# Modulation product: float32 matmuls against two rounded passes of split weights with stacked condition columns

## The chip, the cores and the metric

The kernel runs on one core of one Trainium2 chip. The metric is the device time of one execution in microseconds (us). The time before is the median of three runs, 3209.94 us (3209.03 to 3211.54).

## The reference, cut to what matters

The reference is a stack of transformer-like layers over 256 latent tokens and 256 context tokens of width 1024 (neighbourhood attention with mLSTM, RWKV, MLPs, and further blocks). The part at issue is the modulation of each of the first two layers:

```python
def modulate(x, shift, scale):
    return rms_norm(x) * (1.0 + scale) + shift

def adaln(cond, w, b):          # w: 1024 x 6144, one per layer
    return jnp.split(jax.nn.silu(cond) @ w + b, 6, axis=-1)
```

There are two conditions, `c` and `c_ctx`, so the product per layer is 2 x 1024 times 1024 x 6144. Its six pieces are shift, scale and gate of the mixer and of the MLP. Only the first layer's first 2048 columns (shift and scale of the mixer) are needed at the start; the rest is needed from the output projection of the first mixer on.

## The kernel before, in words

**Weights.** All weights pass through a ring of three slabs in SBUF (`ring`, 128 x 4096 each), filled by SyncE's queue in the order of the list `slabs`; a slab is loaded when the one three places ahead is used (L3308). A slab of the modulation is 1024 x 512: eight k of 128 rows. Layer 0 has 12 of them (`plan_ada(0, 0, 4)`, then behind the eight slabs of the input projection `plan_ada(0, 4, 8)`), layer 1 has 12.

**The modulation product.** `ada_matmuls` (L798) is a generator that a caller advances with `fill(pe, queue, n)`. One step is one k of one slab: a float32 matmul with the silu of the conditions as the stationary operand (8, 16 or 24 columns: the two condition columns stand in a field of zeros, `csil`, so that slab i writes rows 2i and 2i+1 of one PSUM bank) and 512 columns of weights moving (L812). The profile records such a float32 matmul as two. There are three parts (`ADA_PARTS`, L794): part 0 is layer 0's first four slabs, part 1 its other eight, part 2 layer 1's twelve. When a part is done, ScalarE copies the rows (`ada_rows_act`, L830), TensorE turns them by transposes (`ada_turn_pe`, L841), DVE copies them into `modcol` (L851), and GpSimd stores the rows to DRAM (`ada_store_pool`, L860) from which the gates are loaded as broadcasts.

**Where the steps stand.** Part 0 stands at the start, around the first norms (L3321 on). Part 1 is filled in two steps at a time behind each of the 32 units of the two attentions, `na` (16 neighbourhood units of 512 keys) and `cx` (16 context units of 256 keys). Then follow 24 steps of part 2 in one go (L3335), and its other 72 are filled into the mLSTM stage (`ml_pe`, L1442), two behind each S and two behind each of its 32 steps.

**Attention.** Each engine runs the units in software-pipelined ticks (`unit_tick`): in tick i TensorE does scores of unit i (L1086), the turn of unit i-2 (L1094), values of unit i-3 (L1106), and the fill; DVE does the maximum of unit i (L1128 and L1130, with bias L1143, L1138 and L1147) and normalises unit i-1 (L1155, L1159); ScalarE does the exponential of unit i (L1186), copies unit i-2 (L1205) and puts out unit i-3 (L1237). Each engine works its own list strictly in the order written.

**Between.** The softplus of the gates (`softplus_act`, L1308) starts a chain of small scans on DVE (`decay_dve`), exponentials (`decay_act`), transposes and small matmuls (`decay_pe`, L1379 and L1385), then the transposes of q and k and the mLSTM.

**mLSTM.** Four heads. A head starts with the score matrix S (L1449), two broadcasts M (L1455), the decay matrices on DVE (L1506) and their exponentials, masks and weights (L1514, L1518). Then eight steps (four chunks in two directions) follow: three matmuls each on TensorE (L1466, L1467, L1469), and on DVE the state update (L1534, for the first three chunks) and the output (L1537 to L1554). Into the last head DVE and ScalarE split the first slab of the output projection (L1664, L1669).

**Rounded passes.** The other products of the stage are already done with rounded float32: ScalarE copies a slab into a rounded `high`, DVE subtracts to get a rounded `low` in the ring's place, and TensorE does three rounded matmuls where the float32 one stood (`ab_high_act` L911, `ab_low_dve` L916, `ab_in_pe` L954).

Of the kernel before, what the change touches and what calls it, by code (L numbers as in the profile page):

```python
# [1 line left out]

# [5 lines left out]
ALU = mybir.AluOpType  # L8
# [6 lines left out]
P = 128  # L15
# [15 lines left out]
def constant_blocks():  # L31
# [6 lines left out]
        "ident": p == f,  # L38
        "headones": (p // 64) == (f // 64),
# [67 lines left out]
def bidir_dual_stack(nc, a, out, scratch_mod, scratch_rpb, noted):  # L107
    const_at, n_const = constant_columns()

    with ExitStack() as ctx:  # L110
# [592 lines left out]
        csil = area(23136, KT, 46)  # L703
        pad = arena[0:56, 23000:23127]
# [16 lines left out]
        def setup_pool(pool):  # L721
            nc.gpsimd.memset(csil, 0.0).then_inc(*up(pool, "csil zero"))
            pool.wait_ge(*latest(pool))
            nc.gpsimd.dma_start(x[:, :, :], a["x"][0].rearrange("(t p) d -> p t d", p=P))\
                .then_inc(landing("x"), 16)
            nc.gpsimd.dma_start(cx[:, :, :], a["ctx"][0].rearrange("(t p) d -> p t d", p=P))\
                .then_inc(landing("ctx"), 16)
            for part, (layer, n0, ns, base) in enumerate(ADA_PARTS):
                for v in range(2):
                    nc.gpsimd.dma_start(adab[base + v:base + 2 * ns:2, :],  # L730
                                        a["ada_b"][layer, 512 * n0:512 * (n0 + ns)].rearrange("(i f) -> i f", f=512))\
                        .then_inc(landing(f"ada_b {part}"), 16)
# [37 lines left out]

        def setup_pe(pe):
# [14 lines left out]
        def setup_act(act):  # L786
            act.wait_ge(*when(("read", ("vec", 1))))
            act.wait_ge(*when("csil zero"))
            for i, name in enumerate(("c", "c_ctx")):
                nc.scalar.activation(csil[:, :, 22 + i], colB[:, ROWS_B[name]:ROWS_B[name] + 8], ACT.Silu).then_inc(*up(act, "silu c"))  # L790
                act.wait_ge(*latest(act))


        ADA_PARTS = ((0, 0, 4, 64), (0, 4, 8, 32), (1, 0, 12, 0))  # L794
        ADA_BANK = (2, 6, 0)

        def ada_matmuls(pe, part):
            layer, n0, ns, base = ADA_PARTS[part]  # L798
            rows = psum[0:2 * ns, ADA_BANK[part], :]
# [5 lines left out]
            at = slice(base, base + 2 * ns)  # L805
            nc.tensor.matmul(rows, ident[at, at], adab[at, :], start=True, stop=False)
            for i in range(ns):
                name = (f"ada{layer}", n0 + i, 0)
                for k in range(KT):
                    stage(pe, "ada")  # L810
                    s = slab(pe, name)
                    ins = nc.tensor.matmul(rows, csil[:, k, 22 - 2 * i:22 - 2 * i + 2 * ns], s[:, k, :],  # L812
                                           start=False, stop=(i == ns - 1 and k == KT - 1))
                    if k == KT - 1:
                        event = ("ada", "full", part) if i == ns - 1 else None
                        ins.then_inc(*up(pe, event))
# [2899 lines left out]
```

## Time and profile before

| | before |
|---|---|
| median of three runs | 3209.94 us |
| the profiled execution: its own time | 3208.53 us |
| its span | 3206.7 us |
| TensorE busy (matmuls) | 3001.3 us, 94% |
| DVE busy | 1740.6 us, 54% |
| ScalarE busy | 1084.0 us, 34% |
| GpSimd busy | 315.8 us, 10% |
| DMA | 409.30 MB, mean 128 GB/s |

The profile is of one execution, whose own time is 1.4 us under the median. The span is what the profiler saw of it. The stages at issue, in us from the span's start: start and first modulation part to 52, input projection to about 219, `na` units from 224 to 304, `cx` units to 362, scans and turns to about 402, mLSTM to 525, merge and output projection to about 583. Matmuls overlap in the records, so the distance between starts, not the duration, is what one costs in a row.

### The profile page before, as it was taken

How to read it: one execution, taken by the hardware profiler on the slowest of the kernel's cores; microseconds unless marked ns; L12 is line 12 of the kernel's file. 1: busy time of each engine (PE TensorE's matmuls, PEld its weight loads, DVE VectorE, ACT ScalarE, POOL GpSimd, SP SyncE). 2: the span in 40 equal slices, each digit the busy share in tenths (PEclk: the TensorE clock that was granted, in tenths of full speed). 3: DMA queues.
4: the chain of work that ended last, by engine and by line, in shares of the span. 5: the costliest groups of instructions: out<-in, count | busy, mean ns of one | idle time of the engine just before them, and what ended most of it. 6: DMA issues, size and time to landing. Idle time of an engine off the chain costs nothing. (4 is left out here: it accounts for less than half of the span.)

```text
span 3206.7 us, 55619 instructions
## 1 busy us (share of the span) xinstructions
PE 3001.3 (94%) x24656; PEld 2366.2 (74%) x24656; DVE 1740.6 (54%) x2730; ACT 1084.0 (34%) x1704; POOL 315.8 (10%) x421
## 2 busy tenths in 40 slices
PE   7999988999998978898989999999899999998999
PEld 3864335899985458888949989865699898455898
DVE  3334367656554057878735555445655554565553
ACT  2233302334331234344223343423443333143432
POOL 2320011000000032323210000000000000200000
PEclk9999999999999989999989999999899999999999
DMA  8323534355553010000044555543245555413353
GB/s 260 100 105 105 184 131 140 124 184 185 193 176 119 26 28 3 3 3 3 19 143 158 191 164 181 185 147 131 80 158 178 176 185 172 151 60 131 101 183 138
DMA packets 250489, 409.30 MB, mean 128 GB/s; under 512 B 10455, under 2 KB 103016, under 8 KB 250120
## 3 DMA queue, kind: packets, MB, share of 16 engines
q1 hardware_dynamic: 245128, 390.39, 35.8%
q0 software_dynamic: 5120, 15.35, 1.9%
q8 instruction: 194, 3.18, 0.4%
q14 instruction: 47, 0.39, 0.0%
HBM read 400.67 MB, written 2.95 MB: 126 GB/s over the span
## 5 line engine op out<-in xcount | busy, mean ns | idle before, releaser
L350 DVE TENSOR_TENSOR ring_parts<-ring,arena_parts 128x2048 fp32r<-128x2048 f32 (+1 forms) x262 | 580.2, 2255 | 276.9 <-ACT arena_parts L343 274.4
L343 ACT CAST arena_parts<-ring 128x2048 fp32r<-128x2048 f32 (+1 forms) x262 | 480.5, 1885 | 521.7 <-PE psum L2701 229.5
L2701 PE MATMUL psum<-arena_parts 128*128 128x256 f32 x2816 | 513.4, 285 | 2.1 <-DVE arena_parts L575 1.7
L2701 PEld LDWEIGHTS psum<-arena_parts 128*128 128x128 f32 x2816 | 444.6, 194 | 3.5 <-DVE arena_parts L575 2.8
L2701 PE MATMUL psum<-arena_parts,ring_parts 128*128 128x256 f32 x1408 | 401.2, 285 | 0.0
L387 PE MATMUL psum<-arena_parts 128*128 128x512 f32 x1024 | 327.1, 393 | 2.0 <-DVE arena_parts L575 2.0
L2701 PEld LDWEIGHTS psum<-arena_parts,ring_parts 128*128 128x128 f32 x1408 | 273.3, 194 | 0.0
L1737 PE MATMUL psum<-arena_parts 128*128 128x512 f32 x768 | 236.8, 389 | 0.0
L387 PEld LDWEIGHTS psum<-arena_parts 128*128 128x128 f32 x1024 | 193.9, 190 | 42.9 <-DVE arena_parts L575 2.7
L387 PE MATMUL psum<-ring_parts,arena_parts 128*128 128x512 f32 x560 | 219.6, 392 | 0.0
L1719 PE MATMUL psum<-arena_parts 128*128 128x256 f32 x1024 | 195.6, 294 | 5.3 <-issue 3.2
L812 PE MATMUL psum<-ring,arena 128*24 128x512 f32 (+2 forms) x384 | 185.9, 618 | 2.6 <-DMA ring<-in_ada_w 2.6
L1719 PEld LDWEIGHTS psum<-arena_parts 128*128 128x128 f32 x1024 | 166.5, 200 | 9.6 <-issue 6.1
L1737 PEld LDWEIGHTS psum<-arena_parts 128*128 128x128 f32 x768 | 143.4, 188 | 29.0
L2732 DVE TENSOR_TENSOR sc<-sc,psum 128x512 f32<-128x512 f32 x44 | 30.2, 687 | 226.0 <-PE psum L2701 226.0
L1737 PE MATMUL psum<-ring_parts,arena_parts 128*128 128x512 f32 x384 | 149.4, 389 | 0.0
L1719 PE MATMUL psum<-arena_parts,ring_parts 128*128 128x256 f32 x512 | 148.8, 291 | 0.0
L498 POOL TENSOR_SCALAR stat<-stat 128x1 f32<-128x1 f32 x26 | 9.0, 347 | 1327.2 <-ACT sc L489 1327.2
L3202 PE MATMUL psum<-ring,hT 128*128 128x512 f32 x256 | 126.0, 622 | 1.0 <-DMA ring<-in_xmem_wkv 1.0
L387 PEld LDWEIGHTS psum<-ring_parts,arena_parts 128*128 128x128 f32 x560 | 106.3, 190 | 22.4
L2325 PE MATMUL psum<-ring,hT 64*64 64x64 f32 x2560 | 106.8, 234 | 16.1 <-POOL ring L2296 11.8
L2325 PEld LDWEIGHTS psum<-ring,hT 64*64 64x64 f32 x2560 | 99.3, 149 | 17.4 <-POOL ring L2296 11.9
(466 smaller groups left out, 5596.3 us busy)
## 6 DMA issues: line engine op xcount, KB each, us to landing
ring<-in_mlp_w SPq DMA_DIRECT2D x48, 2048.0 KB, 8.3
ring<-in_ada_w SPq DMA_DIRECT2D x24, 2048.0 KB, 7.9
ring<-in_ffn_pre_w_gu SPq DMA_DIRECT2D x44, 1024.0 KB, 6.9
ring<-in_ffn_post_w_gu SPq DMA_DIRECT2D x44, 1024.0 KB, 7.0
ring<-in_ffn_pre_w_down SPq DMA_DIRECT2D x8, 2048.0 KB, 7.8
ring<-in_xmem_wkv SPq DMA_DIRECT2D x8, 2048.0 KB, 7.9
ring<-in_ffn_post_w_down SPq DMA_DIRECT2D x8, 2048.0 KB, 7.9
ring<-in_ab_w_in SPq DMA_DIRECT2D x7, 2048.0 KB, 7.7
```

The lines of the kernel that those rows point to most:

```text
L343: nc.scalar.copy(high_view(name)[:, k, :], raw_view(name)[:, k, :]).then_inc(*up(act, ("high", name, h)))
L350: nc.vector.tensor_tensor(low_view(name)[:, k, :], raw_view(name)[:, k, :], high_view(name).bitcast(F32)[:, k, :], ALU.subtract)\
L387: ins = nc.tensor.matmul(psum[:, b, :], lhs[q][:, k0 + k, P * t:P * t + P], s[:, k, :], start=(k0 + k == 0 and i == 0), stop=(k0 + k == kt ...
L498: nc.gpsimd.tensor_scalar(s[:, 4 + t:5 + t], s[:, 2 * t:2 * t + 1], s[:, 2 * t + 1:2 * t + 2], EPS, ALU.add, ALU.add).then_inc(*up(pool))
L812: ins = nc.tensor.matmul(rows, csil[:, k, 22 - 2 * i:22 - 2 * i + 2 * ns], s[:, k, :], start=False, stop=(i == ns - 1 and k == KT - 1))
L1719: ins = nc.tensor.matmul(psum[:, b, 256 * j:256 * j + 256], s[:, k, at:at + P], src[q][:, k, :], start=(k == 0 and i == 0), stop=(k == 7 a ...
L1737: ins = nc.tensor.matmul(psum[:, b, :], hid_groups[g % 2][q][:, k, P * t:P * t + P], s[:, k, :], start=(g == 0 and k == 0 and i == 0), sto ...
L2325: ins = nc.tensor.matmul(psum[h, b, 64 * c:64 * c + 64], B[left][z][h, c, :], B[right][z][h, c, :], start=True, stop=True)
L2701: ins = nc.tensor.matmul(psum[:, b, 256 * j:256 * j + 256], s[:, k, at:at + P], x_parts[q][:, k, :], start=(k == 0 and i == 0), stop=(k == ...
L2732: nc.vector.tensor_tensor(t, t, psum[:, 2 * (n % 2) + 1, :], ALU.mult)\
L3202: ins = nc.tensor.matmul(psum[:, 6 + i, :], hT[:, k, 256 + P * i:256 + P * i + P], s[:, k, :], start=(k == 0), stop=(k == KT - 1))
```

## The change

The product of parts 1 to 3 is made of rounded weights, in two passes (high and low). The silu is split too, and its high and low columns are stacked: four stationary columns per slab instead of two (`csil_parts`), so that each slab writes four rows, and a small matmul with a constant 0/1 matrix `pairsum` adds the pairs and turns them at once. Part 0 keeps its float32 matmuls. Layer 1's slabs are regrouped: its first four are now part 2, its last eight part 3. A step is now a quarter slab (two k): ScalarE copies the quarter into one of four (later two) buffers, DVE subtracts, TensorE does four matmuls. 48 quarters (12 slabs) go into the attentions, alternately one and two behind a unit; 32 quarters (8 slabs) into the mLSTM stage, one behind each step; the 24 steps between are gone.

```diff
+        ADA_PARTS = ((0, 0, 4, 0), (0, 4, 8, 32), (1, 0, 4, 0), (1, 4, 8, 64))
+        ADA_BANK = (2, 6, 7, 0)
+        ADA_FIRST = (None, 0, 32, 48)
...
+        def ada_high_act(act, g):
+            held = stages[act.name]
+            stage(act, "ada_split")
+            act.wait_ge(*when(("slab", slab_at[ada_slab(g)])))
+            if g < 4:
+                act.wait_ge(*when(("qk", "turned", 7)))
+            elif g < 48:
+                act.wait_ge(*when(("ada quarter", g - 4)))
+            elif g < 50:
+                act.wait_ge(*when("gate columns full"))
+            else:
+                act.wait_ge(*when(("ada quarter", g - 2)))
+            nc.scalar.copy(ada_high_at(g), ada_quarter(raw_view, g)).then_inc(*up(act, ("ada high", g)))
+            stage(act, held)
+        def ada_low_dve(dve, g):
...
+            dve.wait_ge(*when(("ada high", g)))
+            nc.vector.tensor_tensor(ada_quarter(low_view, g), ada_quarter(raw_view, g),
+                                    ada_high_at(g).bitcast(F32), ALU.subtract).then_inc(*up(dve, ("ada low", g)))
+        def ada_ahead(u):
+            return range(min(48, 3 * u // 2 + 4), min(48, 3 * (u + 1) // 2 + 4))
+        def ada_each(u):
+            return 3 * (u + 1) // 2 - 3 * u // 2
...
+                        for j in range(2):
+                            for w in (high, low):
+                                ins = nc.tensor.matmul(rows, csil_parts[:, 2 * q + j, live], w[:, j, :], start=False,
+                                                       stop=last and j == 1 and w is low)
```

The turn of a part, the sum of its pairs for the store in DRAM, and where the splits stand in the lists of the engines:

```diff
-                ins = nc.tensor.transpose(psum[:, b, 2 * ns * j:2 * ns * j + 2 * ns], adab[at, P * j:P * j + P], ident[at, at])
+                ins = nc.tensor.matmul(psum[:, b, 2 * ns * j:2 * ns * j + 2 * ns], adab[at, P * j:P * j + P],
+                                       cst("pairsum")[at, 0:2 * ns], start=True, stop=True)
...
+        def ada_sum_pe(pe, part, b):
...
+            nc.tensor.matmul(psum[0:2 * ns, b, :], cst("pairsum")[at, 0:2 * ns], adab[at, :], start=True, stop=True)\
+                .then_inc(*up(pe, ("sum", "full", part)))
...
             def out(i):
                 att_out(act, key, units, i)
+                if split is not None:
+                    for g in ada_ahead(split + i):
+                        ada_high_act(act, g)
...
+                for g in range(48 + 8 * h, 56 + 8 * h):
+                    ada_high_act(act, g)
+                    if g in (75, 77):
+                        ab_out_high_act(act, 0, g // 77)
+                        stage(act, "ml")
...
                         b = 4 + z + 2 * (j % 2)
+                        ada_low_dve(dve, 48 + 8 * h + 2 * j + z)
```

TensorE's, ScalarE's and DVE's lists:

```diff
-            att_pe(pe, "na", na, [("read", ("qkT", i)) for i in range(8)], ada[1], 2)
-            att_pe(pe, "cx", cxa, (), ada[1], 2)
-            fill(pe, ada[1], 1)
-            fill(pe, ada[2], 24)
+            ada_next = chain(ada[1], ada[2])
+            att_pe(pe, "na", na, [("read", ("qkT", i)) for i in range(8)], ada_next, ada_each)
+            att_pe(pe, "cx", cxa, (), ada_next, ada_each)
+            fill(pe, ada_next, 1)
+            ada_turn_pe(pe, 1, 2)
+            ada_turn_pe(pe, 2, 3)
+            ada_sum_pe(pe, 1, 0)
...
-            att_act(act, "na", na, 0.125, [("ab_in", "full", 6, 3)])
-            att_act(act, "cx", cxa, 0.125)
-            ada_rows_act(act, 1)
+            att_act(act, "na", na, 0.125, [("ab_in", "full", 6, 3)], split=0)
+            att_act(act, "cx", cxa, 0.125, split=16)
             softplus_act(act)
+            for part in (1, 2):
+                ada_rows_act(act, part)
+            ada_sum_act(act, 1, 0)
...
-            att_dve(dve, "na", na, 0.125, after_first=["bias ready"])
-            att_dve(dve, "cx", cxa, 0.125)
+            att_dve(dve, "na", na, 0.125, after_first=["bias ready"],
+                    split=lambda i: ([i] if i < 4 else []) + (list(ada_ahead(i - 3)) if i >= 3 else []))
+            for g in ada_ahead(13):
+                ada_low_dve(dve, g)
+            att_dve(dve, "cx", cxa, 0.125, split=lambda i: ada_ahead(14 + i))
```

In the attentions DVE's `split(i)` stands behind the normalisation of unit i, which is in tick i+1; ScalarE's high copies stand behind the output of unit i, in tick i+3 (and those of quarters 0 to 3 behind the first four exponentials). In `ml_pe` the fill behind S is gone and the one behind each step is one quarter. `decay_out_dve` is followed by the `modcol` copies of parts 1 and 2, the turn of part 3 with its sum stands where both turns stood, ahead of the second half of the output projection. At the start, `x` is loaded ahead of the memset of `csil`, `adab` is cleared and its bias rows loaded for parts 0, 1 and 3 (part 2's later, `late_bias_pool`), the silu goes to `stat` and is split by ScalarE and DVE. The buffer `pad` of the position bias moves to another place, for which ScalarE waits ahead of the outputs of one projection slab that the bias rows have been written.

## Rows read from the trace of the kernel before

**Rows 1.** The page: busy us of each engine, share of the span, instructions.
```profile
PE 3001.3 (94%) x24656; PEld 2366.2 (74%) x24656; DVE 1740.6 (54%) x2730; ACT 1084.0 (34%) x1704; POOL 315.8 (10%) x421
```
**Rows 2.** Busy by stretch: length, PE, PEld, DVE, ACT, POOL, clock, DMA share, GB/s.
```profile
120.00:160.00 40.00, 40.00 (x174) 32.35 (x173) 17.75 (x19) 11.95 (x12) 14.00 (x16) 1.00 0.17 55
240.00:291.00 51.00, 51.00 (x202) 20.81 (x200) 24.03 (x55) 17.05 (x44) 5.05 (x12) 0.99 0.24 83
312.75:353.50 40.75, 40.75 (x145) 14.51 (x144) 13.67 (x50) 12.38 (x48) 0.00 (x0) 1.00 0.35 118
362.40:383.20 20.80, 20.79 (x49) 4.87 (x48) 15.43 (x45) 3.52 (x5) 1.15 (x2) 1.00 0.86 301
404.70:525.00 120.30, 109.36 (x377) 44.54 (x376) 84.32 (x278) 12.25 (x13) 17.07 (x25) 0.94 0.41 141
535.60:544.90 9.30, 4.81 (x25) 3.36 (x25) 8.57 (x24) 6.34 (x17) 2.23 (x4) 0.61 0.17 62
```
**Rows 3.** Timeline, neighbourhood attention, DVE: start us, us, engine, line, operation [idle before].
```profile
246.49 0.42 DVE L1143 SCALAR_TENSOR_TENSOR sc<-psum,arena 128x256 f32<-128x256 f32 x1 [2.16 <-PE psum L1086]
...
248.33 0.49 DVE L1159 TENSOR_SCALAR sc<-sc,stat 128x512 f32<-128x512 f32 x1
250.97 0.42 DVE L1143 SCALAR_TENSOR_TENSOR sc<-psum,arena 128x256 f32<-128x256 f32 x1 [2.15 <-PE psum L1086]
```
**Rows 4.** Timeline, context attention, one tick of all engines.
```profile
312.75 0.70 PE L1086 MATMUL psum<-arena 64*128 64x256 f32 x2
...
313.55 0.42 DVE L1128 TENSOR_REDUCE stat<-psum 128x1 f32<-128x256 f32 x1 [4.04 <-PE psum L1086]
...
314.19 0.47 ACT L1186 ACTIVATE sc<-psum,stat 128x256 f32<-128x256 f32 x1 [4.24 <-DVE stat L1130]
314.32 1.89 PE L812 MATMUL psum<-ring,arena 128*16 128x512 f32 x4
314.39 0.35 DVE L1159 TENSOR_SCALAR sc<-sc,stat 128x256 f32<-128x256 f32 x1
...
314.66 0.36 ACT L1205 COPY sc<-psum 128x256 f32<-128x256 f32 x1
314.91 0.26 ACT L1237 COPY hT<-psum 64x128 f32<-64x128 f32 x1
316.14 0.70 PE L1086 MATMUL psum<-arena 64*128 64x256 f32 x2
```
**Rows 5.** Timeline, mLSTM stage, DVE in one step and the next one's start.
```profile
418.83 0.35 DVE L1534 SCALAR_TENSOR_TENSOR sc<-sc,psum 128x129 f32<-128x129 f32 x1 [0.60 <-PE psum L1469]
...
420.57 0.35 DVE L1554 SCALAR_TENSOR_TENSOR arena<-sc,stat,arena 128x128 f32<-128x128 f32 x1
...
421.52 0.35 DVE L1534 SCALAR_TENSOR_TENSOR sc<-sc,psum 128x129 f32<-128x129 f32 x1 [0.60 <-PE psum L1469]
```
**Rows 6.** Timeline, mLSTM stage, DVE from the start of the second head.
```profile
435.33 2.16 DVE L1506 TENSOR_SCALAR arena<-psum,sc 128x128 f32<-128x128 f32 x8 [3.29 <-PE psum L1455]
...
440.82 0.35 DVE L1534 SCALAR_TENSOR_TENSOR sc<-sc,psum 128x129 f32<-128x129 f32 x1
```
**Rows 7.** Lines L916 and L911, the splits of the input projection: duration ns min/median/max, shapes.
```profile
L916 DVE TENSOR_TENSOR ring_parts<-ring,sc_parts x7: 2291/2292/2293, 47.1 to 184.3; 128x2048 fp32r<-128x2048 f32 x7
L916 DVE TENSOR_TENSOR ring_parts<-ring,ring_parts x1: 1226/1226/1226, 182.5 to 182.5; 128x1024 fp32r<-128x1024 f32 x1
...
L911 ACT CAST ring_parts<-ring x1: 1050/1050/1050, 181.4 to 181.4; 128x1024 fp32r<-128x1024 f32 x1
```
**Rows 8.** Timeline: the last fill and the softplus, and two turns on TensorE.
```profile
359.62 1.89 PE L812 MATMUL psum<-ring,arena 128*16 128x512 f32 x4
...
362.15 0.63 ACT L1308 ACTIVATE arena<-arena 4x512 f32<-4x512 f32 x1
...
391.03 3.55 PE L1385 MATMUL psum<-arena,const 4*128 4x4 f32 x16
...
52.04 0.41 PE L841 MATMUL psum<-const,adab 8*128 8x8 f32 x4 [0.66 <-ACT adab L830]
```

More of the change, by code:

```diff
@@ L769, in bias_pool, with ada_bias_pool, late_bias_pool @@
             pool.wait_ge(*latest(pool))
+        def ada_bias_pool(pool, part):
+            layer, n0, ns, base = ADA_PARTS[part]
+            for v in range(2):
+                nc.gpsimd.dma_start(adab[base + v:base + 4 * ns:4, :],
+                                    a["ada_b"][layer, 512 * n0:512 * (n0 + ns)].rearrange("(i f) -> i f", f=512))\
+                    .then_inc(landing(f"ada_b {part}"), 16)
+        def late_bias_pool(pool):
+            stage(pool, "bias")
+            layer, n0, ns, base = ADA_PARTS[2]
+            pool.wait_ge(*when(("mod", "turned", 0)))
+            nc.gpsimd.memset(adab[base:base + 4 * ns, :], 0.0).then_inc(*up(pool))
+            pool.wait_ge(*latest(pool))
+            ada_bias_pool(pool, 2)
         def setup_pe(pe):
@@ L808, in ada_matmuls @@
                 name = (f"ada{layer}", n0 + i, 0)
-                for k in range(KT):
+                live = slice(28 - 4 * i, 28 - 4 * i + 4 * ns)
+                for q in range(4):
                     stage(pe, "ada")
[L811 to L816, printed above, removed]
-                        now[("used", slab_at[name])] = (f"ada_by_{pe.name}", count[f"ada_by_{pe.name}"])
+                    last = i == ns - 1 and q == 3
+                    if part == 0:
+                        s = slab(pe, name)
+                        for k in (2 * q, 2 * q + 1):
+                            ins = nc.tensor.matmul(rows, csil[:, k, live], s[:, k, :], start=False, stop=last and k == 7)
+                    else:
+                        g = ADA_FIRST[part] + 4 * i + q
+                        pe.wait_ge(*when(("ada low", g)))
+                        high, low = ada_high_at(g), ada_quarter(low_view, g)
+                        for j in range(2):
+                            for w in (high, low):
+                                ins = nc.tensor.matmul(rows, csil_parts[:, 2 * q + j, live], w[:, j, :], start=False,
+                                                       stop=last and j == 1 and w is low)
+                    if part or q == 3:
+                        ins.then_inc(*up(pe, ("ada", "full", part) if last else None))
+                        here = (f"ada_by_{pe.name}", count[f"ada_by_{pe.name}"])
+                        if part:
+                            now[("ada quarter", g)] = here
+                        if q == 3:
+                            now[("used", slab_at[name])] = here
                     yield
@@ L1112, in att_pe, with att_dve @@
                 if queue is not None and step is values:
-                    fill(pe, queue, each)
-        def att_dve(dve, key, units, scale, probs=True, after_first=(), mem_after={}, rows=None):
+                    fill(pe, queue, each if isinstance(each, int) else each(i))
+        def att_dve(dve, key, units, scale, probs=True, after_first=(), mem_after={}, rows=None, split=None):
             stage(dve, "att")
@@ L1166, in att_dve @@
                     stage(dve, "att")
+                if step is normalise and split is not None:
+                    for g in split(i):
+                        ada_low_dve(dve, g)
                 if step is normalise and rows is not None and i in (5, 7):
@@ L1171, in att_dve, with att_act @@
                     out_low_dve(dve, rows, k, 2)
-        def att_act(act, key, units, scale, needs=(), rows=None):
+        def att_act(act, key, units, scale, needs=(), rows=None, split=None):
             stage(act, "att")
@@ L3321, in _ @@
             setup_pe(pe)
-            ada = [ada_matmuls(pe, part) for part in range(3)]
-            fill(pe, ada[0], 16)
+            ada = [ada_matmuls(pe, part) for part in range(4)]
+            fill(pe, ada[0], 8)
             first_turn_pe(pe, "L0a")
-            fill(pe, ada[0], 8)
+            fill(pe, ada[0], 4)
             first_turn_pe(pe, "C0a")
-            fill(pe, ada[0], 8)
+            fill(pe, ada[0], 4)
             fill(pe, ada[0], 1)
```

93 lines of the change are left out of this document (63 added, 30 removed).

## The prediction

> **What bounds the kernel now.** I read the page first: TensorE is busy 94% of the span, VectorE (DVE) 54% [rows 1]. That is a mean over stages, so the second view was the busy time by stretch. The change acts between 224 and 545 us of the span, and the stretches there differ [rows 2]. In both attentions and in the mLSTM stage TensorE is (nearly) always busy and DVE waits; between 362 and 383 us TensorE works off 24 modulation steps while the decay scans on DVE set the pace. The third view was the timeline of one period of each stage. A neighbourhood unit repeats every 4.48 us, with DVE idle for 2.15 of them [rows 3]. A context unit repeats every 3.39 us, of which 1.82 are the two modulation steps [rows 4]. An mLSTM step repeats every 2.69 us, of which 1.71 are two modulation steps, and DVE idles only 0.60 [rows 5]. So what matters is how much TensorE time goes and how much DVE time comes, stage by stage, against idle times of 2.15, 2.2 and 0.60 us.
>
> **Prices.** An old step is two records of 0.43 us (49 in 20.8 us) [rows 2]: 0.86 us. A rounded matmul of 512 columns costs 0.23 us (174 in 40 us) [rows 2], so a quarter slab (two k, high and low: four matmuls) costs 0.92 us where its two old steps cost 1.71. All 20 slabs free 63 us of TensorE. Each quarter adds a rounded copy of 128x1024 on ScalarE, 1.05 us, and a subtraction of 128x1024 on DVE, 1.226 us [rows 7]. In a row of instructions a subtraction takes between 1.04 (its columns alone: 2291 less 1226 ns for 1024) and 1.26 (its duration and the 0.04 between dependent instructions of [rows 5]). I take 1.15, since neighbours don't depend on it. 80 of them are 92 us of DVE.
>
> **Neighbourhood attention.** DVE per unit is 2.38 us (246.49 to 248.33, and 0.49 and the gap) and 1.5 subtractions: 4.1 us. TensorE is 4.48 less 1.82 and plus 1.38: 4.0 us. DVE becomes the pace, narrowly: 0.37 less a unit over 11 steady units, -4.1 us. The last units, where TensorE is alone, save 2.0 (four fills of 1.82 against six quarters); the start at half clock, where ScalarE has four early copies ahead of its own work, saves 0.6. Sum -6.7 us (-8 to -4).
>
> **Context attention.** This is the part that decides. DVE's list for tick t is maximum t, normalise t-1, then the subtractions of `ada_ahead(14 + t - 1)`. ScalarE's is exponent t (waits for maximum t), copy t-2, output t-3, then the high copies of `ada_ahead(16 + t - 3)`: the same quarters. In the first attention DVE asks for them one tick later (`i - 3`); here in the same tick. So maximum t+1 stands behind a subtraction, which waits for a high copy, which stands behind exponent t, which waits for maximum t: a ring through two in-order engines. From [rows 4]: maximum to exponent 0.64, to the copy 0.47, to the output 0.25, its 0.26, then 1.05 for the high copy and about 0.06 of signals: 2.74 us a tick, and 1.15 for each subtraction. Ticks with one quarter take 3.9 us, with two 5.0. Thirteen such ticks with 19 quarters are 57.5 us; the three ahead of them about 6.6, the end (normalise, turn, values, one quarter) 3.1: 67 us, where sixteen units took 54.2 and about 0.9 for a cold start. +12 us. If the ring didn't bind, DVE's own work would be 1.2 and 1.73, 3.0 a unit, and the stage would gain 4.
>
> **Between the stages.** The 24 steps at 362 us go, 20.8 us of TensorE, and bring nothing: DVE's scans (15.4 us busy in that stretch) [rows 2] and the exponentials after them hide them. Into that cover come the row copies, turns and sum of parts 1 and 2, an estimated 8 us of TensorE even at half clock; without the scans they would cost those 8. The softplus no longer waits for the last fill and the row copy: 359.62 to 362.15 [rows 8] becomes about 0.4, -2.1 us. The fill between the first S and M goes, on the path into the first head: -1.8 us.
>
> **mLSTM.** TensorE per step falls to 0.86 and 0.92, 1.8 us. DVE's list per step is 2.1 us (418.83 to 420.57, and 0.35) [rows 5] and one subtraction: 3.25. 32 steps, less 0.38 in the eight that update no state: 101 us. DVE's work at a head's start is 5.5 (435.33 to 440.82) [rows 6], four times 22; four `cat` remainders 2.9; two `ab_out` remainders 4.5; at three head changes DVE waits some 0.3 for M, 1 in all. 131.4 us against 120.3 [rows 2]: +11.1 us (+7 with 1.04 a subtraction, +15 with 1.26). ScalarE's copies are no term: each waits for the quarter two before it and has over 2 us to spare. Behind the new waits on DVE nothing stands but the state update, needed by TensorE two steps on.
>
> **Edges.** The turns become full matmuls. Eight such took 3.55 us at half clock, 0.44 each, so about 0.22 at full clock: four cost 0.9 against 0.41 for the first transposes [rows 8], +0.5. Ahead of the second half of the output projection stand turns and a sum of 512 columns, in a stretch at clock 0.61 [rows 2], of which part would else run cold: +1.0 (0 to 2). TensorE enters `ab_out` later beside DVE's merge: +0.3. Setup (x issued ahead of the memset, four bias loads for six, another memset) lies before the first slab has landed: 0. The late bias load and the wait for the bias rows come tens of us before anyone needs them: 0. Slabs are used every 10 to 13 us, where the old fills used one in 6.9 without a stall (8 steps at 0.86, the stretch from 362.4 of rows 2): 0.
>
> **Clock.** With TensorE idle a third of the time in two stages some of it will run at 1.2 GHz. The mLSTM stage shows 0.94 at 91% busy, the first attention 0.99 at full [rows 2]. At half clock throughout, a context tick costs 5.7 instead of 4.5 and an mLSTM step 3.6 instead of 3.1: 34 us. I take 2 (0 to 34).
>
> **Sum:** -6.7 + 12 - 2.1 - 1.8 + 11.1 + 0.5 + 1.0 + 0.3 + 2 = +16.3 us. The profiled execution took 3208.53 us (span 3206.7), 1.4 under the median of 3209.94; I add to the median: 3226 us.
>
> **Rivals.**
> - *The ring doesn't bind*: some cover lets the high copies run ahead, and DVE's throughput sets the context attention. Then that part is -4 and the sum 0: 3210 us. For it, ScalarE is idle 70% there; against it, the order of both lists. 0.12.
> - *Faster: the subtraction runs at the rate of one-source operations.* L1159 takes 0.49 us for 512 columns [rows 3] and 0.35 for 256 [rows 4], 0.55 ns a column, which makes 0.77 for 1024, 0.69 in a row. 51 subtractions on the path (32 and 19) save 0.46 each, 23 us: 3203 us. It decides below 0.83 us a subtraction, and is faster beyond noise only below 0.71. Against it, the same kind of instruction shows 1.226 [rows 7]. With smaller ways to gain, 0.09.
> - *Half clock*: TensorE's gaps of 1 to 2 us in each tick keep it at 1.2 GHz for most of both stages: 3258 us, for half of them 3241. For it, the clock is already 0.61 in the stretch that is half idle [rows 2]; against it, work at half clock fills the gaps. 0.12.
> - *No cheaper matmul*: with few stationary columns a rounded matmul takes 0.43 us like a half of the old. A quarter is then 1.7 us, a neighbourhood unit 5.2 instead of 4.1, 16 us more, and the other stages hide it: 3242 us. 0.05.
>
> On the second rival: the trace shows 1.20 ns a column for two tensors. The Trainium skill (VectorE: DVE Perf Modes, "Why `tensor_tensor` can't do 2×_2P or 4×") says that the doubled mode spends the second read port on the same tensor, so an operation of two tensors can't have it. By that rule this rival falls away; the trace agrees. On the third: the Trainium skill (TensorE: Matmul & The Clock Gate, "A second HAM failure mode: psum-queue depth-cycling") tells of a kernel whose short idle times between groups of matmuls made the clock swing. By that rule the time would lie nearer to 3241; no run here shows it yet.
>
> **How the numbers follow.** My case has 0.60 and a range of its own of 3217 to 3237. With the ring's rival at 3210 and half of the clock's at 3241 the range is 3208 to 3242; outside stay the faster case and the full half clock. A measurement tells about 0.2%, 6.4 us. Faster: 0.09. Within: the ring's rival and the low end of mine, 0.16. Slower: 0.75.
>
> **What would show it.** Right: context ticks of 3.9 and 5.0 us in turn, DVE waiting for ScalarE's high copy about 1.5 us in each, softplus some 4 us later than 362; the mLSTM stage 131 us with DVE over 90% busy; neighbourhood units of 4.1 us. Wrong: context ticks near 3.0 (no ring), mLSTM steps of 2.7 or less (cheap subtractions) or 3.6 with a clock near 0.5, and anything moved behind the output projection, where both traces should run alike.

## The result and the profile after

The changed kernel takes 3228.0 us (median of four runs, 3227.9 to 3231.7) against 3209.5 us for the kernel before beside it (3208.7 to 3211.5): ratio 1.006, 95% interval 1.0048 to 1.0072. It is 18.5 us slower; the forecast was 16.3 us slower.

The profiled execution of the changed kernel is the longest of its four, 3231.74 us (span 3229.9), 3.7 us over their median; experiment 2 shows where such a difference can lie. The page's busy times, and the group of all new subtractions (busy, mean ns; idle time before them):

```profile
PE 2964.4 (92%) x24682; PEld 2384.8 (74%) x24682; DVE 1833.4 (57%) x2813; ACT 1165.9 (36%) x1788; POOL 326.0 (10%) x425
...
L853 DVE TENSOR_TENSOR ring_parts<-ring,arena_parts 128x1024 fp32r<-128x1024 f32 x80 | 97.5, 1234 | 26.8 <-ACT arena_parts L846 25.1
```

TensorE lost 36.9 us of busy time and VectorE gained 92.8 [rows 1]; the span grew all the same. Busy time by stretch, to be read against [rows 2] (length, PE, PEld, DVE, ACT, POOL, granted clock, DMA share, GB/s). The four are the neighbourhood attention, the ring part of the context attention, the scans, the mLSTM:

```profile
224.00:302.40 78.40, 75.80 (x325) 37.95 (x324) 64.87 (x105) 52.34 (x93) 22.36 (x39) 0.87 0.41 142
309.00:371.00 62.00, 53.35 (x186) 22.30 (x185) 36.15 (x74) 32.91 (x74) 0.00 (x0) 0.78 0.39 136
375.40:396.40 21.00, 6.19 (x26) 3.25 (x23) 15.42 (x45) 6.85 (x9) 1.14 (x2) 0.60 0.41 147
415.20:547.20 132.00, 81.22 (x362) 50.92 (x361) 120.84 (x310) 43.87 (x44) 21.32 (x24) 0.86 0.32 112
```

In the context attention no engine is full: TensorE 86%, VectorE 58%, ScalarE 53%. In the mLSTM VectorE is at 92%, TensorE at 62%; before, VectorE was at 70% and TensorE at 91% [rows 2]. The same points in both traces, the first row in us from the span's start, show where the time came from. A unit's maximum is the first instruction of VectorE on it, the first D is the first decay matrix of the mLSTM, and the merge is what follows its last step:

| from ... to | before | after | difference | forecast |
|---|---|---|---|---|
| start to first maximum of `na` | 225.5 | 224.7 | -0.8 | +0.5 |
| first maximum of `na` to that of `cx` | 79.5 | 77.8 | -1.7 | -6.7 |
| first maximum of `cx` to softplus | 57.1 | 72.9 | +15.8 | +12 - 2.1, and 2 for the clock |
| softplus to first D | 42.6 | 39.8 | -2.8 | -1.8 |
| first D to merge | 120.2 | 132.1 | +11.9 | +11.1 |
| merge to the end | 2681.7 | 2682.6 | +0.9 | +1.3 |

The sum, taken before rounding, is 23.2 us in these two executions, 4.7 more than between the medians.

One tick of the context attention, VectorE and ScalarE alone (start us, us, engine, line, operation [idle before <- who ended it]):

```profile
327.72 0.42 DVE L1228 TENSOR_REDUCE stat<-psum 128x1 f32<-128x256 f32 x1
...
328.36 0.47 ACT L1289 ACTIVATE sc<-psum,stat 128x256 f32<-128x256 f32 x1 [2.07 <-DVE stat L1230]
328.56 0.35 DVE L1259 TENSOR_SCALAR sc<-sc,stat 128x256 f32<-128x256 f32 x1
...
329.08 0.26 ACT L1345 COPY hT<-psum 64x128 f32<-64x128 f32 x1
329.24 1.05 ACT L846 CAST arena_parts<-ring 128x1024 fp32r<-128x1024 f32 x1
330.39 1.23 DVE L853 TENSOR_TENSOR ring_parts<-ring,arena_parts 128x1024 fp32r<-128x1024 f32 x1 [1.48 <-ACT arena_parts L846]
331.53 0.42 DVE L1228 TENSOR_REDUCE stat<-psum 128x1 f32<-128x256 f32 x1
```

ScalarE idles 2.07 us for VectorE's maximum and VectorE 1.48 us for ScalarE's high copy. This is the chain of the forecast. The tick is 3.81 us, where it was 3.39 us in [rows 4]. The next lines are VectorE in two mLSTM steps and the start of a third. VectorE shows no idle time at all (0.60 us a step in [rows 5]), and the steps take 3.19 and 3.39 us:

```profile
453.11 1.23 DVE L853 TENSOR_TENSOR ring_parts<-ring,arena_parts 128x1024 fp32r<-128x1024 f32 x1
454.25 0.34 DVE L1646 SCALAR_TENSOR_TENSOR sc<-sc,psum 128x129 f32<-128x129 f32 x1
...
456.30 1.23 DVE L853 TENSOR_TENSOR ring_parts<-ring,arena_parts 128x1024 fp32r<-128x1024 f32 x1
...
459.69 1.23 DVE L853 TENSOR_TENSOR ring_parts<-ring,arena_parts 128x1024 fp32r<-128x1024 f32 x1
```

### The profile page after: what moved, and what is told of

Read it like the earlier page. It is cut to its first block and busy times, and to the rows that moved or that the text cites. A ratio compares the mean times of both kernels' runs of the same rounds, so it can differ in the third digit from the quotient of the medians.

```text
span 3229.9 us, 55857 instructions
## 1 busy us (share of the span) xinstructions
PE 2964.4 (92%) x24682; PEld 2384.8 (74%) x24682; DVE 1833.4 (57%) x2813; ACT 1165.9 (36%) x1788; POOL 326.0 (10%) x425
## 5 line engine op out<-in xcount | busy, mean ns | idle before, releaser
L389 PEld LDWEIGHTS psum<-arena_parts 128*128 128x128 f32 x1024 | 192.9, 189 | 42.6 <-DVE arena_parts L577 2.7
L2437 PE MATMUL psum<-ring,hT 64*64 64x64 f32 x2560 | 104.4, 230 | 17.1 <-POOL ring L2408 11.9
L853 DVE TENSOR_TENSOR ring_parts<-ring,arena_parts 128x1024 fp32r<-128x1024 f32 x80 | 97.5, 1234 | 26.8 <-ACT arena_parts L846 25.1
```

Source lines behind the costliest of these rows:

```text
L389: ins = nc.tensor.matmul(psum[:, b, :], lhs[q][:, k0 + k, P * t:P * t + P], s[:, k, :], start=(k0 + k == 0 and i == 0), stop=(k0 + k == kt ...
L853: nc.vector.tensor_tensor(ada_quarter(low_view, g), ada_quarter(raw_view, g), ada_high_at(g).bitcast(F32), ALU.subtract).then_inc(*up(dve, ...
L2437: ins = nc.tensor.matmul(psum[h, b, 64 * c:64 * c + 64], B[left][z][h, c, :], B[right][z][h, c, :], start=True, stop=True)
```

## The experiments

**1. The ring opened (`cx_later`).** One edit in VectorE's list: in the context attention the subtractions that make the low parts (the remainders) come one tick later.

```diff
             for g in ada_ahead(13):
                 ada_low_dve(dve, g)
-            att_dve(dve, "cx", cxa, 0.125, split=lambda i: ada_ahead(14 + i))
+            att_dve(dve, "cx", cxa, 0.125, split=lambda i: ada_ahead(13 + i) if i else ())
+            for g in ada_ahead(29):
+                ada_low_dve(dve, g)
```

> In the context attention VectorE subtracts each quarter's remainder one step of the loop later than in the changed kernel (the remainders of a tick no longer wait for the high copies that ScalarE makes in the same tick), everything else as in the changed kernel. Theory (the ring through VectorE and ScalarE paces the ticks at 3.8 and 4.9 us): the ticks fall to what the busiest engine needs, VectorE's 1.5 x 1.23 + 1.3 = 3.2 us a tick, so the stretch from the fourth maximum to the last normalisation falls from 62.3 to about 44 us and the whole by 12 to 19 us, to 3209 to 3216. Rival A (TensorE at half clock paces it, not the ring): TensorE was busy 53.4 of 62.0 us there at a mean granted clock of 0.78, so no more than 9 us can go, to about 3220 or above. Rival B (the time is paid again later, in the softplus and the gate rows that follow): the attention falls, the whole stays at 3228.

Measured: 3212.4 us (11 runs, 3206.9 to 3215.8), ratio to the kernel before 1.0001 (0.9992 to 1.001): 15.6 us under the changed kernel. The stretch from the fourth maximum to the last normalise fell from 62.3 to 41.0 us, and first maximum to softplus from 72.9 to 48.8. The stretch in the trace:

```profile
307.20:347.90 40.70, 40.70 (x185) 18.56 (x185) 37.55 (x75) 32.34 (x73) 0.00 (x0) 1.00 0.65 226
```

TensorE is busy throughout, at full clock: 40.7 us of busy time in place of 53.4 for the same matmuls (185 and 186 records). The difference, 12.7 us, is what the half clock had cost in busy time. In one tick of it the subtraction no longer waits, and ScalarE waits 0.17 us for the maximum where it waited 2.07:

```profile
326.42 0.47 ACT L1289 ACTIVATE sc<-psum,stat 128x256 f32<-128x256 f32 x1 [0.17 <-DVE stat L1230]
326.62 0.35 DVE L1259 TENSOR_SCALAR sc<-sc,stat 128x256 f32<-128x256 f32 x1
...
327.05 2.36 DVE L853 TENSOR_TENSOR ring_parts<-ring,arena_parts 128x1024 fp32r<-128x1024 f32 x2
```

It follows that the order of one list made the context attention's loss. The stretch differs between executions, but not by so much: with the ring open it took 41.0, 42.5 and 45.1 us in the other three profiled executions (`hybrid_again`, `hybrid_start`, `hybrid`, granted clock 1.00, 0.97 and 0.91), with the ring closed never less than 59.3. Rival A is out: its bound of 9 us took TensorE's busy time for fixed, but the half clock went with the waits. Rival B is out in the stages that follow: first D comes 24.2 us earlier, and so does the merge. Between the two profiled executions 24.1 us are left at the merge and 18.3 at the end; 3.5 of the difference goes between 1240 and 1620 us of the span, where the two kernels run the same instructions. It is of the size of the spread between executions: from the merge to the end one and the same kernel took 2682.8 us in `hybrid` and 2686.2 in `hybrid_again`. What it comes from is open.

**2. More work for TensorE in the same ring (`cx_high_twice`).** The added passes spoil the product; they are a load and nothing else.

```diff
-                            for w in (high, low):
+                            for w in ((high, high, low) if 24 <= g < 48 else (high, low)):
```

> In the context attention each high pass is issued twice, so a quarter has 6 matmuls in place of 4 (the product of that part is then not the reference's; a load on TensorE alone). It asks whether TensorE fell to half clock there because it had too little to do. Theory (the ring leaves TensorE idle, its clock falls, and the half clock costs about 4 us): with 48 more matmuls of 0.21 us at full clock the mean granted clock of the stretch rises from 0.78 to over 0.95, the ticks come down to the ring's 3.8 and 4.9 us and the stretch of 62.3 us stays or falls to about 58. Rival (the clock does not follow the load so closely, TensorE is the bound at half clock): 48 matmuls of 0.43 us make the stretch longer by 10 to 20 us.

Measured: 3227.0 us in one run. From the fourth maximum to the last normalise, where the changed kernel took 62.3 us:

```profile
303.60:364.20 60.60, 55.07 (x222) 23.90 (x221) 36.18 (x74) 33.00 (x73) 0.00 (x0) 0.89 0.40 139
```

Half again as many passes, and the stretch is no longer than before: TensorE was not the bound, and the rival's 10 to 20 us did not come. The last ticks alternate between 3.81 or 4.07 and 5.16 or 5.21 us. The granted clock is 0.89 against 0.78, not the 0.95 of the theory, and whether the added passes raised it is not shown. The changed kernel's own instructions were profiled in this stretch three times more, in `part3_float`, `ml_half_one_source` and `ml_half_gpsimd`, whose edits act later: 59.4, 59.3 and 62.3 us, at 0.87, 0.87 and 0.77. The first of them:

```profile
309.64:369.00 59.36, 47.93 (x186) 20.75 (x185) 36.41 (x74) 32.95 (x74) 0.00 (x0) 0.87 0.41 142
```

So 60.6 us at 0.89 lies within what the kernel does without the added passes. What these executions do show is the price of the clock in the ring: the three ticks from the ninth maximum on take 17.4 us at 0.60 in the changed kernel's profile and 14.5 at 0.98 in `part3_float`, 2.9 us that are there in two executions of four. The three unprofiled executions of the changed kernel are 3.6 to 3.8 us shorter than its profiled one, which would fit with the shorter form, but they left no trace.

**3. No remainders at all (`no_low`).**

```diff
-                        pe.wait_ge(*when(("ada low", g)))
+                        pe.wait_ge(*when(("ada high", g)))
...
-                            for w in (high, low):
+                            for w in (high,):
...
         def ada_low_dve(dve, g):
...
-            nc.vector.tensor_tensor(ada_quarter(low_view, g), ...
```

> All remainders and their passes are left out (the modulation product from the high parts alone, so 2 matmuls a quarter and no subtraction); the high copies stay. It shows by stage what the remainders cost. By my theory: neighbourhood attention from 4.16 us a unit to about 3.7 (TensorE's own work and ScalarE's copies), 5 to 8 us less in the stage; context attention without the ring, ticks about 3 us, 15 us less or more; mLSTM steps from 3.25 to 2.1 us, 32 x 1.15 = 37 us less; about 55 to 60 us in all, 3168 to 3173. Rival (the cost lies in the waits on the high copies and in the half clock): mLSTM falls by less than 20 us and the context attention by less than 6, since less matmul work also lowers the clock, 3190 or above.

The product is then made of the high parts alone. Measured: 3151.1 us in one run, 77 under the changed kernel, where 55 to 60 were expected. The context attention (fourth maximum to last normalise) and the mLSTM (first D to merge):

```profile
294.50:327.00 32.50, 31.46 (x144) 14.49 (x144) 14.45 (x55) 31.06 (x72) 0.00 (x0) 1.00 0.83 291
...
371.30:466.20 94.90, 66.58 (x325) 49.50 (x324) 84.18 (x279) 45.66 (x45) 14.85 (x24) 0.82 0.50 175
```

The mLSTM falls by 37.3 us, 1.16 for each of 32 subtractions: the price of 1.15 taken in the forecast, on the path in full. The low passes are gone too, but they are not what counts there: `hybrid` below puts TensorE's work back in another form, and the stage takes 93.7 us. The first maximum of `na` to that of `cx` falls from 77.8 to 65.4 us, more than the 5 to 8 expected: the units alternate between 3.25 and 3.70 us, which is 7.0 of it, the start gives 3.3 and the end 2.1. From there to the softplus it falls by 33.0 us, where 15 or more were expected. How subtractions and passes share in these two was not tested. The rival is out.

**4. Half of the mLSTM's remainders on GpSimd (`ml_half_gpsimd`).**

```diff
-                        ada_low_dve(dve, 48 + 8 * h + 2 * j + z)
+                        if z == 0:
+                            ada_low_dve(dve, 48 + 8 * h + 2 * j + z)
...
                         pool.wait_ge(*latest(pool))
+                for g in range(49 + 8 * h, 56 + 8 * h, 2):
+                    ada_low_pool(pool, g)
```

`ada_low_pool` is `ada_low_dve` with `nc.gpsimd.tensor_tensor`.

> In the mLSTM every second quarter's remainder (those of the backward steps, 16 of 32) is subtracted by GpSimd instead of VectorE. Theory (VectorE paces the 32 steps at 3.25 us and each subtraction costs it 1.15 us on the path): the stretch from the first D to the merge falls by 16 x 1.15 = 18 us, from 132.1 to about 114, and the whole to about 3210. Rival A (VectorE is not the pace, TensorE's wait on the state is): nothing moves, 3228. Rival B (GpSimd's subtraction slows VectorE's own instructions while both run, or is itself late): GpSimd takes about 2.5 us for one (10.1 us for 4096 elements a row in the trace of the kernel before), four a head, 10 of about 30 us; if VectorE's instructions beside it grow by a fifth, 18 us shrink to about 5 to 10, 3218 to 3223.

Measured: 3245.8 us (four runs, 3240.4 to 3246.7), ratio 1.0104 (1.0089 to 1.012): 18 us slower than the changed kernel, where no theory went above 3228. First D to merge is 145.6 us instead of 132.1, and these 13.5 us are all but 0.5 of what lies between the two profiled executions. Timeline, GpSimd and VectorE:

```profile
470.75 0.16 DVE L1669 RECIPROCAL stat<-stat 128x1 f32<-128x1 f32 x1
...
470.91 2.34 POOL L861 TENSOR_TENSOR ring_parts<-ring,arena_parts 128x1024 fp32r<-128x1024 f32 x1 [2.34 <-ACT arena_parts L846]
470.95 2.45 DVE L1677 SCALAR_TENSOR_TENSOR arena<-sc,stat,arena 128x128 f32<-128x128 f32 x1
473.43 1.22 DVE L853 TENSOR_TENSOR ring_parts<-ring,arena_parts 128x1024 fp32r<-128x1024 f32 x1
```

The sum into the arena, 0.35 us otherwise, takes 2.45 and ends 0.15 us after GpSimd's subtraction. Over the stage three of VectorE's kinds of instruction grew by more than 0.2 us, all with two operands in SBUF: the subtraction by 8.9, the sum into the arena by 8.4 and the 128x1 comparison by 7.0 us, 24.3 together (the text recorded ahead of experiment 5 has 22.6). That is more than the 16 x 1.23 us that GpSimd took over, but by 4.6 us only. Besides, VectorE now waits 10.0 us for TensorE ahead of its state updates, where it waited 0.3, and the granted clock of the stage is 0.74 instead of 0.86; what of that follows from what was not separated. Those of the steps that read PSUM kept their durations to 0.01 us. The Trainium skill (SBUF — State Buffer, "SBUF: two separate sides") says that VectorE and GpSimd share a port pair that one of them holds for a whole instruction, and that a VectorE instruction with two inputs in SBUF needs it, but only against a GpSimd instruction that reads SBUF. By that rule rival B was the one to expect, and larger than I priced it; the trace agrees.

**5. The same with one source on GpSimd (`ml_half_one_source`).**

```diff
-            nc.gpsimd.tensor_tensor(ada_quarter(low_view, g), ada_quarter(raw_view, g),
-                                    ada_high_at(g).bitcast(F32), ALU.subtract)
+            nc.gpsimd.tensor_scalar(ada_quarter(low_view, g), ada_quarter(raw_view, g),
+                                    0.0, None, ALU.mult)
```

> As ml_half_gpsimd, but GpSimd multiplies the raw quarter by 0 in place of subtracting the high part (one source in SBUF in place of two; the low passes of those quarters then add nothing). It asks what held VectorE up in ml_half_gpsimd, where three of its kinds of instruction grew and no other: the subtraction (median 1.23, up to 3.26 us), the 128x1 comparison (0.16, up to 1.40) and the sum into the arena (0.35, up to 2.45), each with two operands in SBUF, 22.6 us together. Theory (a VectorE instruction with two operands in SBUF is shut out while GpSimd reads SBUF at all): the same three kinds still grow, for as long as the shorter GpSimd instruction lasts, the stretch from first D to merge ends between 114 and 146 us. Rival (only two readers of two sources each collide): no instruction of VectorE grows, and the stretch falls to about 114 us, the whole to about 3210.

The low parts of these quarters are then zero. Measured: 3226.5 us in one run; first D to merge 127.0 us, 5.1 less than in the changed kernel. GpSimd and VectorE in two places:

```profile
432.48 3.06 POOL L861 TENSOR_SCALAR ring_parts<-ring 128x1024 fp32r<-128x1024 f32 x1 [2.34 <-ACT arena_parts L846]
...
434.17 0.16 DVE L1667 TENSOR_TENSOR stat<-stat,sc 128x1 f32<-128x1 f32 x1
...
434.56 1.05 DVE L1674 TENSOR_SCALAR arena<-sc,stat 128x128 f32<-128x128 f32 x1
...
437.88 3.69 POOL L861 TENSOR_SCALAR ring_parts<-ring 128x1024 fp32r<-128x1024 f32 x1 [2.35 <-ACT arena_parts L846]
...
440.21 0.35 DVE L1677 SCALAR_TENSOR_TENSOR arena<-sc,stat,arena 128x128 f32<-128x128 f32 x1
```

My theory falls for the short instructions. The comparison at 434.17 and the sum at 440.21, each with two operands in SBUF, run at their usual 0.16 and 0.35 us in the middle of GpSimd's instruction. What is held up is VectorE's one-source instruction from SBUF to SBUF (L1674): 0.29 us otherwise, here 1.05, ending with GpSimd's at 435.6. It grew by 3.0 us in all. Whether GpSimd's subtraction holds it up too is not shown: in `ml_half_gpsimd` none of them began inside one. Of the two-operand ones only the long ones grew: the first subtraction of each head, begun 0.42 us after GpSimd's instruction, takes 1.69 us and ends 0.66 before it, and a subtraction of 128x2048 for the output projection takes 3.12 us instead of 2.28. It holds in the other direction too: GpSimd's instruction takes 2.77 us at its shortest and 3.69 at 437.88, where VectorE's subtraction had begun just before it. The same section of the Trainium skill has a VectorE instruction with two inputs in SBUF blocked by any GpSimd instruction that reads SBUF, for its full length; on this point the measurement differs. The stretch did not come down to the rival's 114 either. GpSimd's one-source instruction takes 3.16 us on average, not 2.59, and TensorE waited for it 11 times, 9.2 us; how the rest divides stays open.

**6. The last part back to float32 (`hybrid`, `part3_float`).** `hybrid` has the edit of `cx_later`, and part 3 is multiplied as in the kernel before, in 64 steps of one k, placed as follows; `part3_float` has the same without the edit of `cx_later`.

```diff
-                    if part == 0:
+                    if part in (0, 3):
...
             fill(pe, ada_next, 1)
+            fill(pe, ada[3], 6)
             ada_turn_pe(pe, 1, 2)
             ada_turn_pe(pe, 2, 3)
-            ada_sum_pe(pe, 1, 0)
+            ada_sum_pe(pe, 1, 4)
+            fill(pe, ada[3], 14)
             decay_pe(pe)
...
                     nc.tensor.matmul(psum[:, 2 + z, :], sel[0:4, h, :], gm[0:4, z, :], ...
+                fill(pe, queue, 3)
...
-                for g in range(48 + 8 * h, 56 + 8 * h):
-                    ada_high_act(act, g)
...
-                        ada_low_dve(dve, 48 + 8 * h + 2 * j + z)
```

> The context attention as in cx_later, and the last part of the modulation product (the eight slabs multiplied beside the mLSTM) goes back to 64 float32 matmuls on the raw slabs: no high copies, no remainders there; 6 of them right after the attention, 14 ahead of the gate columns, 3 in each head's wait for its masks and one in each step. Theory (the changed kernel's mLSTM is paced by VectorE's 32 subtractions, and the kernel before it by TensorE's 72 float32 matmuls of 0.85 us): with 32 to 44 of these and no subtraction neither binds, the stretch from the first D to the merge falls from 132 to what no_low showed without remainders, 95 us; the softplus to D stretch grows by 0 to 3; the whole is 3212 - 37 + 2 = 3177 (3172 to 3185). Rival (TensorE's float32 matmul in each step lies on the state's path, since VectorE waits for the product behind it): 32 x 0.85 = 27 us come back, about 122, 3204.

> The changed kernel with the last part alone put back to float32 (as in hybrid), the context attention's ring left in. If ring and mLSTM are separate costs, it stands above hybrid by what cx_later gained over the changed kernel, 16 us: about 3193. Rival (part of the gain of one was given back by the other, by way of the slab loads): the difference is under 10 us.

Measured: `hybrid` 3170.7 us (3168.7 to 3171.6), ratio 0.9877 (0.9861 to 0.9894), and once more on another occasion (`hybrid_again`, below) 3170.0, ratio 0.9869 (0.9855 to 0.9884). That is 39 us under the kernel before and 57 under the changed one. `part3_float` 3188.1 us (3186.4 to 3192.2), ratio 0.9935 (0.992 to 0.995), 17.4 above `hybrid`, where 16 was expected: ring and mLSTM are separate costs. First D to merge is 93.7 us; its stretch, and the period of VectorE's steps:

```profile
392.50:483.50 91.00, 84.97 (x332) 38.88 (x331) 82.06 (x269) 13.13 (x13) 15.14 (x24) 0.98 0.35 122
```
```profile
424.39 0.35 DVE L1647 SCALAR_TENSOR_TENSOR sc<-sc,psum 128x129 f32<-128x129 f32 x1
...
426.52 0.35 DVE L1647 SCALAR_TENSOR_TENSOR sc<-sc,psum 128x129 f32<-128x129 f32 x1
...
428.66 0.35 DVE L1647 SCALAR_TENSOR_TENSOR sc<-sc,psum 128x129 f32<-128x129 f32 x1
```

A step is 2.13 us, VectorE's own list, with one float32 step of TensorE inside it. Both engines are over 90% busy. The rival's 27 us did not come. The whole is 1.3 us under the range expected, and softplus to first D fell by 2.9 us (1.4 in `hybrid_again`) from `cx_later` where it was to grow by 0 to 3.

**7. The start of the neighbourhood attention (`hybrid_start`, beside `hybrid_again`).**

```diff
-                    split=lambda i: ([i] if i < 4 else []) + ...
+                    split=lambda i: ([2 * i - 4, 2 * i - 3] if i in (2, 3) else []) + ...
```

> As hybrid, with the first four remainders of the neighbourhood attention moved behind its third and fourth normalise instruction (two each), in place of one behind each of the first four. Theory (the neighbourhood attention missed its forecast of 6.7 us because each of the first subtractions, 1.36 us beside GpSimd's rotation, stands ahead of the next maximum): the distance from the first to the fourth row maximum falls from 8.9 to what it was in the kernel before, 7.3 us or less, the end of the attention comes 1.3 to 2.7 us earlier, and the whole is 3168 to 3169.5. Rival (TensorE at half clock, not VectorE, sets these units): the first distances shrink, the fifth or sixth maximum comes when it came, and the whole stays at 3170.7.

> The kernel of hybrid once more, on the same chip as hybrid_start, as its yardstick: 3170.7 us within 1.5 us, and a stretch from the first row maximum of the neighbourhood attention to its last of 65 to 66 us.

Measured: 3170.6 us (3168.7 to 3173.3) against 3170.0 (3163.8 to 3172.6). From the first to the fourth unit 7.24 us instead of 8.90; the next two take 8.57 and 6.59 instead of 7.98 and 6.02, and the whole `na` series of maxima 63.6 instead of 64.5 (65 to 66 was expected for `hybrid_again`). The subtractions do stand in the way of the first maxima, but moving them saves 0.9 us in the stage, which is less than the 1.1 between `hybrid` and `hybrid_again`, one kernel, and nothing that the time shows: mostly the rival.

## Why the prediction was right, point by point

- **The sign and the size were right, and two of its terms carry them.** The ring was forecast from the order of two lists with a chain of 2.74 us and 1.15 for each subtraction, 3.9 and 5.0 us a tick; the shortest ticks are 3.81 and 4.94. `cx_later` shows the ring to be the cause, by opening it and nothing else. The rival in which the ring doesn't bind was priced at 3210 us, the kernel without it takes 3212.4.
- **The mLSTM** was +11.1 by the forecast and is +11.9 us. The step is 3.2 to 3.4 us, TensorE waits for VectorE's subtraction 27 times, 39.8 us together, and `no_low` gives 1.16 us for a subtraction where 1.15 was taken. That price also rules out the rival of the cheap subtraction: it measures 1.23 us, as in [rows 7]. The rival of the dear matmul is out as well: the four passes of a quarter start 0.23 us apart in `cx_later` (326.61 to 327.31 us), as the forecast took them.
- **The neighbourhood attention** is the term that was mis-sized: -1.7 us instead of -6.7. Its steady part holds: units alternate 4.63 and 3.70, mean 4.16 against 4.1, and from the sixth to the sixteenth maximum 3.2 us are saved (4.1 forecast for one unit more). What failed is "the start at half clock [...] saves 0.6": up to the sixth maximum the start took 23.8 us where it had taken 21.0, a loss of 2.8. I had looked at ScalarE's early copies and not at VectorE's early subtractions, which stand ahead of the second, third and fourth maxima and took 1.36 us there instead of 1.23:

```profile
228.70 1.36 DVE L853 TENSOR_TENSOR ring_parts<-ring,arena_parts 128x1024 fp32r<-128x1024 f32 x1
229.98 0.41 DVE L1243 SCALAR_TENSOR_TENSOR sc<-psum,arena 128x256 f32<-128x256 f32 x1
```

  `hybrid_start` shows that they explain 1.7 us of the first units but little of the time: the fifth and the sixth maximum wait for TensorE, 4.27 and 1.81 us, which is at half clock up to 246 us of the span. How long that lasts differs between executions. First to sixth maximum before, in the changed kernel, and in `cx_high_twice`, which has the changed kernel's instructions up to there (length, PE, PEld, DVE, ACT, POOL, granted clock, DMA share, GB/s):

```profile
225.50:246.50 21.00, 19.31 (x50) 6.70 (x49) 10.30 (x24) 5.85 (x15) 17.51 (x38) 0.67 0.05 17
```
```profile
224.70:248.50 23.80, 21.27 (x53) 8.76 (x52) 16.93 (x28) 12.70 (x22) 21.05 (x36) 0.57 0.04 15
```
```profile
224.20:243.50 19.30, 17.16 (x56) 7.56 (x54) 16.84 (x28) 12.43 (x22) 17.19 (x28) 0.73 0.05 17
```

  With the clock back earlier the start took 19.3 us, and the whole way from the first maximum of `na` to that of `cx` 72.9 us, 6.6 less than before, where 6.7 was forecast. In the other profiled executions with these instructions it took 76.8 to 78.0. So the term hangs on a length of half clock that the forecast had no row for, and why it differs is open. The end, forecast to save 2.0, saved 1.4 (last maximum of `na` to first of `cx`, 12.8 and 11.4).
- **The context attention** with the softplus came to +15.8 us where +9.9, and 2 for the clock, were forecast. Only the size was off: 13 ticks took 62.3 us, not 57.5. The granted clock was 0.78 there, and where TensorE was slow ScalarE's next high copy waited for a quarter still being multiplied (five times, 4.8 us in this attention). The clock was the term with the widest bounds, 0 to 34 us, taken at 2. 2.9 us of the miss are one more piece at half clock, which two of the four profiled executions don't have (experiment 2). The rule of the Trainium skill (TensorE: Matmul & The Clock Gate, "A second HAM failure mode: psum-queue depth-cycling"), by which 3241 us was more likely, points the right way; the trace agrees in direction, with 0.78 and 0.86 granted in the two stages and 1.00 in the first with the waits gone (`cx_later`), and not in size.
- **Between and at the edges**: softplus to first D -2.8 (-1.8 forecast), merge to the end +0.9 (+1.3). The last is no confirmation: two executions of one kernel differ by 3.3 us there (`hybrid`, `hybrid_again`). The start was 0.8 us earlier instead of 0.5 later, but that is no finding: in `cx_later`, with the same instructions up to there, the first maximum came 1.3 us later than in the changed kernel.

In the order of the table the misses are -1.3, +5.0, +3.9 (with the 2 for the clock), -1.0, +0.8 and -0.4, together 6.9 us before rounding. The profiled execution of the changed kernel was 3.7 us over its median and that of the kernel before 1.0 under its own, so the medians miss by 2.2. That the miss is so small is in part luck: the half clock moves the two attentions by 5.1 and 2.9 us between executions of the same instructions, and the forecast could size neither.

## What to carry to other kernels

Before moving work onto two engines that each run a fixed list, write both lists out for one tick and look for a cycle: a consumer placed in the same tick as its producer closed one here that cost 16 us with no engine over 86% busy, and one tick of slack removed it. Trading 63 us of TensorE for 92 us of VectorE pays only where VectorE idles: in the attentions it did once the ring was open, in the mLSTM, with 0.60 us of idle time a step against a subtraction of 1.15, it did not, and a mix by stage beat both kernels by 39 us or more. A third engine is no free helper for VectorE either: see whether its instructions are held up before counting what is taken off.

## What the runs showed of the hardware that was not expected

- While GpSimd subtracts one SBUF tensor from another (2.59 us in the mean for 128x1024), VectorE's instructions with two SBUF operands wait for its end (0.35 grew to 2.45 us, 0.16 to 1.40, 1.23 to 3.26), and those with a PSUM operand run on. While GpSimd runs a one-source instruction (3.16 us), the two short kinds run on at 0.16 and 0.35 us, the long one grows from 1.23 to 1.69, and a one-source one of 128x128 from SBUF to SBUF waits (0.29 to 1.05).
- GpSimd's one-source multiplication by a constant was slower than its two-source subtraction of the same shape, 3156 against 2590 ns in the mean (2.77 against 2.34 us at the shortest).
- TensorE's granted clock went up from 0.78 to 1.00 in the context attention when the waits between its groups went (`cx_later`).
- The same instructions are granted different clocks in different executions: 0.77 to 0.87 in the context attention with the ring (62.3 to 59.3 us), 0.91 to 1.00 without it (45.1 to 41.0 us), and 0.57 to 0.73 in the first six units of the neighbourhood attention (23.8 to 19.3 us). A few us of a stage can't be put down to an edit on one profile of each kernel.
